# Sampled tokens of both recurrent branches stacked by heads into 128-row blocks, their new states from sequence-masked values in four row groups

## The reference, cut to what matters

```
# GLA:  S_t = diag(a_t) S_{t-1} + k_t^T v_t ; o_t = q_t S_t
o = einsum(qc * exp(b), S) + einsum(A, vc)
S = exp(b_last) * S + einsum('bhsd,bhsv->bhdv', kc * exp(b_last - b), vc)
# GDN:  S_t = g_t (I - b_t k_t k_t^T) S_{t-1} + b_t k_t v_t^T ; o_t = q_t S_t
X = triangular_solve(L, rhs)           # L is 4 x 4 for a sampled sequence
v_new = u - einsum(w, S)
o = einsum(qc * exp(b), S) + einsum(attn, v_new)
S = exp(b_last) * S + einsum('bhsd,bhsv->bhdv', kc * exp(b_last - b), v_new)
```

## Time and profile before

| | |
|---|---|
| timed runs, median | 1013.75 us |
| profiled execution, span from first to last instruction | 1005.3 us |
| profiled execution beyond its span | not on the page; the median is 8.45 us above the span |
| TensorE busy | 919.8 us (91%) |
| VectorE, ScalarE, GpSimd busy | 411.9, 261.1, 64.0 us |
| GLA's sampled states, TensorE 283.0 to 307.1 us | granted clock 0.50 |
| GDN's sampled states, TensorE 593.2 to 617.5 us | granted clock 0.50 |
| DMA | 190.64 MB, mean 190 GB/s |

### The profile page before, as it was taken

The page is one execution under the profiler, slowest core; times in us unless marked ns, Lnnn a source line. Parts: engine busy times, 40 slices in busy tenths (PEclk is TensorE's granted clock), DMA queues, the critical chain, the costliest instruction groups (busy, mean ns, idle before and its releaser), DMA issues.

```text
span 1005.3 us, 13130 instructions
## 1 busy us (share of the span) xinstructions
PE 919.8 (91%) x5070; PEld 640.2 (64%) x5070; DVE 411.9 (41%) x1038; ACT 261.1 (26%) x630; POOL 64.0 (6%) x92
## 2 busy tenths in 40 slices
PE   5989999989989899999999978958999999999994
PEld 3567767767667699878987777746445444544533
DVE  2120015666655864645555477141132232222215
ACT  3121015666603323343335220130110111011012
POOL 0000000000230000000001056000000000000000
PEclk9879999999957999999999975985999999999998
DMA  8945757252438212131216317990799999997621
GB/s 222 348 155 188 244 173 238 93 168 84 126 129 257 76 43 81 47 125 43 84 43 166 100 42 233 339 349 1 266 339 352 372 337 342 345 378 274 223 112 48
DMA packets 134414, 190.64 MB, mean 190 GB/s; under 512 B 6656, under 2 KB 90283, under 8 KB 134309
## 3 DMA queue, kind: packets, MB, share of 16 engines
q1 hardware_dynamic: 134360, 189.89, 55.8%
HBM read 178.93 MB, written 10.95 MB: 189 GB/s over the span
## 4 chain that ended last, share of the span: by engine, by line
PE 83%; DVE 8%; ACT 3%; issue 2%; SPq 1%; DMA 1%; POOL 0%; DVEq 0%; ACTq 0%; POOLq 0%
PE bank L420 80%; PE bank L423 3%; DMA arena<-in_w_ada 1%; DVE arena L1183 1%; DVE arena L1651 1%; DVE arena L1047 1%; ACT arena L1749 0%; SPq L2136 0%; DVE arena L1168 0%; DVE arena L1337 0%; POOL arena L2094 0%; DVE arena L1432 0%; DVE arena L1429 0%; DVE arena L1474 0%; ACT arena L1923 0%
## 5 line engine op out<-in xcount | busy, mean ns | idle before, releaser
L420 PE MATMUL bank<-arena 128*128 128x288 f32 (+10 forms) x4752 | 877.9, 404 | 65.8 <-DVE arena L1071 8.6
L420 PEld LDWEIGHTS bank<-arena 128*128 128x128 f32 (+5 forms) x4752 | 603.7, 176 | 324.7 <-issue 186.3
L1846 ACT ACTIVATE arena<-arena 128x288 f32<-128x288 f32 (+1 forms) x56 | 25.0, 447 | 157.8 <-DVE arena L1168 157.7
L423 PE MATMUL bank<-arena 128*128 128x128 f32 (+6 forms) x318 | 50.8, 293 | 15.4 <-DMA arena<-in_w_conv 7.4
L423 PEld LDWEIGHTS bank<-arena 128*128 128x128 f32 (+6 forms) x318 | 37.0, 151 | 35.6 <-issue 20.1
L1658 DVE TENSOR_TENSOR arena<-arena,bank 128x288 f32<-128x288 f32 x64 | 28.8, 455 | 29.4 <-PE bank L420 27.9
L1183 DVE SCALAR_TENSOR_TENSOR arena<-arena 128x312 f32<-128x312 f32 x72 | 39.5, 549 | 2.5
L1038 DVE TENSOR_TENSOR arena<-bank,arena 128x18 f32<-128x18 f32 x24 | 4.2, 174 | 82.3 <-PE bank L420 82.3
L1638 DVE SCALAR_TENSOR_TENSOR arena<-bank,arena 128x512 f32<-128x512 f32 x8 | 5.5, 692 | 78.0 <-ACT arena L1994 78.0
L1744 ACT ACTIVATE arena<-arena 128x288 f32<-128x288 f32 (+4 forms) x60 | 33.7, 562 | 2.0
L1984 ACT ACTIVATE arena<-bank 128x512 f32<-128x512 f32 x8 | 4.8, 597 | 111.7 <-PE bank L420 111.7
(11 more groups left out here) (204 smaller groups left out, 465.0 us busy)
## 6 DMA issues: line engine op xcount, KB each, us to landing
arena<-in_w_in SPq DMA_DIRECT2D x36, 1024.0 KB, 6.4
arena<-in_w_exp_gate SPq DMA_DIRECT2D x8, 4096.0 KB, 13.9
arena<-in_w_exp_up SPq DMA_DIRECT2D x8, 4096.0 KB, 17.1
arena<-in_w_exp_down SPq DMA_DIRECT2D x8, 4096.0 KB, 12.8
arena<-in_w_ada SPq DMA_DIRECT2D x24, 1024.0 KB, 5.4
arena<-in_state_gla SPq DMA_DIRECT2D x4, 1024.0 KB, 6.4
out_gla_s<-arena SPq DMA_DIRECT2D x4, 1024.0 KB, 6.7
arena<-in_w_out SPq DMA_DIRECT2D x4, 1024.0 KB, 6.0
```

The lines of the kernel that those rows point to most:

```text
L420: return T.matmul(out, lhsT, rhs, start=start, stop=stop)
L423: return T.transpose(out, in_, ident[0:n, 0:n])
L1846: A.activation(sg, sg, ACT.Exp).then_inc(mark("proj_by_scalar", f"sig{s3}"), 1)
```

## The change

Sampled tokens are stacked by heads: row 32h + t of a 128-row block is token t of head h. GLA needs one such block, GDN two (heads 0 to 3 and 4 to 7). VectorE writes the values of tile 2 straight into that form as it drains the transposes. Scores, solve and outputs become full 128 x 128 products under the block mask `tri4`; the gates are stacked once, at step 3 (`stack`). The old states are read as before, but their result is already in the stacked form, so no expansion is needed, and GLA's output product adds onto it in its bank.

New states: not the keys but the values are masked, once per sequence and side by side (`vM` on GpSimd for GLA, `RM` on VectorE for GDN); a product takes 32 rows of keys of one head (rows 32h to 32h+31, so each head has its own row group) and 512 columns of masked values (two GLA or four GDN sequences), and each head has its own bank.

The order changes too. GLA's tile 2 stands at the steps 28, 29, 30, 32 to 35 (four chunks of two sequences), 36 and 37; each chunk reads two sequences' states and updates them at once, and its state block is loaded there, one by one, not four together. GDN's state updates stand in an item of their own, `gdns_states`, behind the turn, at 74.

```diff
-GLA_AT = ((21, 22, 23, 23, 24, 25), (25, 26, 27, 27, 28, 29), (29, 30, 31, 33, 34, 35))
-GDN_AT = (38, 53, 68)
+GLA_AT = ((21, 22, 23, 24, 25), (25, 26, 27, 28, 29))
+GLAS_AT = (28, 29, 30, 32, 33, 34, 35, 36, 37)
+GDN_AT = (38, 53)
+GDNS_AT = 68
+STACK_AT = 3
...
-        elif item == ("gla_states_read", 2):
-            for i in range(4):
-                add(("sgla", i), I["state_gla"][2 * i:2 * i + 2].rearrange("s h k v -> k (s h) v"))
+        elif kind == "glas_chunk":
+            add(("sgla", c), I["state_gla"][2 * c:2 * c + 2].rearrange("s h k v -> k (s h) v"))
...
-                for s in range(NSEQ):
-                    pe.wait_ge(*when(f"kem1 {s}"))
-                    for g in range(2):
-                        b = take(6 + g, f"gla state {s} {g}")
-                        for hh in range(2):
-                            h = 2 * g + hh
-                            last = mm(b[:, 256 * hh:256 * hh + 256], kem1[0:32, s % 2, 128 * h:128 * h + 128],
-                                      vA[0:32, 2, 256 * h:256 * h + 256])
...
+        def glas_decays():
+            pe.wait_ge(*when("wa2"))
+            b = take(4, "gla2 logits read")
+            for h in range(HA):
+                last = mm(b[32 * h:32 * h + 32, 0:DKA], raT[0:RANK + 1, SEQ:TOK],
+                          wa2[0:RANK + 1, DKA * h:DKA * h + DKA])
...
+        def glas_chunk(c):
...
+            for q in range(2):
+                s_ = 2 * c + q
+                for h in range(HA):
+                    mm(pm[6][32 * h:32 * h + 32, 0:DVA], qbM[:, h, 32 * s_:32 * s_ + 32], w[:, q, h, :],
+                       s_ == 0, False)
+            pe.wait_ge(*when(f"vM {c}"))
+            for h in range(HA):
+                b = take((4, 5, 7)[h], f"gla state {c} {h}") if h < 3 else ring_bank(f"gla state {c}")
+                mm(b[:, 0:512], keTa[32 * h:32 * h + 32, 0, :],
+                   vM[32 * h:32 * h + 32, 2 * c:2 * c + 2, :].rearrange("p s v -> p (s v)")) \
+                    .then_inc(mark("gla_products", f"gla state product {c} {h}"), 1)
...
+        def gdns_states():
+            pe.wait_ge(*when("gdn2 ke"))
+            for half in range(2):
+                for g in range(2):
+                    pe.wait_ge(*when(f"RM {half} {g}"))
+                    for j in range(4):
+                        b = take(4 + j, f"gdn state {half} {g} {j}")
+                        mm(b[:, 0:512], ke[32 * j:32 * j + 32, g, :],
+                           RM[2 * half + g][32 * j:32 * j + 32].rearrange("p s v -> p (s v)")) \
+                            .then_inc(mark("gdn_products", f"gdn state product {half} {g} {j}"), 1)
...
+        def glas_scores():
+            pool.wait_ge(*when("gla1 oT1 ready"))
+            pool.wait_ge(*when("vtok7"))
+            for s in range(NSEQ):
+                ins = G.tensor_scalar(vM[:, s, :], vAS, const("seq")[:, s:s + 1], None, ALU.mult)
+                if s % 2:
+                    ins.then_inc(mark("masked_values", f"vM {s // 2}"), 1)
...
+            if name[0] == "sgla":
+                for h in range(HA):
+                    sp.wait_ge(*when(f"gla state {c} {h}"))
+            else:
                 for g in range(2):
-                    sp.wait_ge(*when(f"{name[0][1:]} state {s} {g}"))
+                    for j in range(4):
+                        sp.wait_ge(*when(f"gdn state {c // 2} {g} {j}"))
```

More of the change, by code:

```diff
@@ L334, in used @@
         return f"used {chunk_of[name]}"
[L339 to L343, removed]
+    GLA_PARTS = ("decays", "sums", "scores", "out", "turn")
+    GLAS_PARTS = [("glas_decays",), ("glas_sums",), ("glas_scores",)] + [("glas_chunk", c) for c in range(4)] \
+        + [("glas_out",), ("glas_turn",)]
+    GDN_PARTS = [("gdn_scores",)] + [("gdn_level", lv) for lv in range(LEVELS)] \
+        + [("gdn_values",), ("gdn_out",), ("gdn_turn",)]
+    GDNS_PARTS = [("gdns_scores",), ("gdns_level", 0), ("gdns_level", 1), ("gdns_values",), ("gdns_out",),
+                  ("gdns_turn",), ("gdns_states",)]
     stands_after = {}
@@ L846, in gdn_turn, with gdns_scores @@
                 last.then_inc(mark("gdn_products", t + f"oT{g} ready"), 1)
+        def gdns_scores():
+            pe.wait_ge(*when("gdn2 tg"))
+            b = take(4, "gdn2 D")
+            mm(b[:, 0:2 * P], ones, X2[:, 0:2, :].rearrange("p g t -> p (g t)")) \
+                .then_inc(mark("gdn_products", "gdn2 bc"), 1)
+            pe.wait_ge(*when("gdn2 compact"))
+            b = take(6, "gdn2 KK read")
+            for g in range(2):
+                last = mm(b[:, P * g:P * g + P], kC[:, g, :], kC[:, g, :])
+            last.then_inc(mark("gdn_products", "gdn2 KK"), 1)
+            b = take(5, "gdn2 AT")
+            for g in range(2):
+                last = mm(b[:, P * g:P * g + P], kC[:, g, :], qC[:, g, :])
+            last.then_inc(mark("gdn_products", "gdn2 QK"), 1)
@@ new lines, in gdns_out, with gdns_turn @@
+        def gdns_out():
+            pe.wait_ge(*when("gdn2 vn"))
+            b = take(4, "gdn2 o")
+            for g in range(2):
+                last = mm(b[:, P * g:P * g + P], AT[:, g, :], R[:, g, :])
+            last.then_inc(mark("gdn_products", "gdn2 o ready"), 1)
+        def gdns_turn():
+            pe.wait_ge(*when("gdn2 oN"))
+            b = take(4, "gdn2 oT1")
+            for g in range(2):
+                last = tr(b[:, P * g:P * g + P], Y[:, g, :], P)
+            last.then_inc(mark("gdn_products", "gdn2 oT1 ready"), 1)
@@ L1910, in gla_out, with gdns_out @@
+        def gdns_out():
+            act.wait_ge(*when("gdn2 o"))
+            for g in range(2):
+                last = A.activation(sqo[:, g, :], E[:, g, :], ACT.Square, accum_out=ssum[:, g:g + 1])
+            last.then_inc(mark("gdn_by_scalar", "gdn2 squares"), 1)
+            act.wait_ge(*when("gdn2 squares"))
+            rstd(srs[:, 0:2], ssum[:, 0:2], 1.0 / DVB, "gdn_by_scalar", "gdn2 rstd")
         def gla_out(m):
```

549 lines of the change are left out of this document (340 added, 209 removed).

## The result

The changed kernel takes 963.8 us (median of four runs, 962.3 to 964.3) against 1013.3 beside it: a ratio of 0.952, 95% interval 0.950 to 0.954. The forecast was 967.

What follows compares the result with a forecast made beforehand. TensorE, busy 919.8 of 1005.3 us, was taken as the bound. GLA -30, GDN -1.4 and -15.4, gates and constants +0.3 sum to -46.5: span 958.8, plus 8.45 gives 967 us; 8-in-10 range 957 to 988.

Steps and rivals of the forecast that it cites:

- A chunk: GLA steps 33 to 36, each with a chunk before it: TensorE 6.8 us, VectorE 6.6, four times 6.8 making 27.2.
- The open choice: Chunk state passes: 3.46 us one after the other or 0.87 four at once; 0.87 taken from the column groups.
- the new wait for bank 4: GLA step 28: sampled decays wait until 234.5 for VectorE to empty the bank, with step 29 queued behind.
- the start of the first chunk: GLA after steps 30 to 32: TensorE at 258.5, with nothing won yet against the old kernel.
- the fold's wait for VectorE: GLA steps 30 and 31: GpSimd's masks cost VectorE 2 to 3 us; bound 0 to 2, nothing in the sum.
- GDN's scores: After GLA's step 38: VectorE some 4 us behind from chunk 3; scores start at 299.6, 30 us won.
- GDN to the end of the reads: Sampled GDN from scores until reads: 15.8 us instead of 17.2, 1.4 won; the reads stay at 7.2.
- Behind the reads: GDN's reads to the output projection: 30.4 us instead of 45.8, 15.4 won; updates 17.9 of it.
- rivals 2 and 3: Low clock during GLA's chunks, 995 us, chance 0.06; low clock kept from step 32 on, 1032 us, chance 0.03.
- rival 1: GLA and GDN state products: row groups do not overlap, 20 us more, 987 us; chance 0.13.
- SP's queue: Step 36's weights wait for block 0's store, bound 0 to 2; later GDN stores, bound 0 to 3; both taken 0.
- The added 8.45 us: Whole kernel: median of timed runs above the profiled span, added to the predicted span of 958.8 to give 967.

Runs made afterwards that it cites:

- the experiment on one row group: All heads' state products put on rows 0 to 31 instead of four row groups, against the changed kernel: 991.6 us.
- Chunks together: The four GLA chunks placed together behind step 35 instead of one each behind steps 32 to 35, against the changed kernel: 965.0 us.
- the second execution: The changed kernel run once more, unedited, beside three edited kernels on the same chip: 963.6 us (956.3 to 964.2).
- the experiment on the masks: ScalarE instead of GpSimd masks the values of GLA's sampled tokens, against the changed kernel: 960.5 us.
- the output product at 37: GLA's sampled output product behind step 37 instead of 36, its turn behind 38 instead of 37, against the changed kernel: 961.4 us.
- fillers: 22 full-height products of constants put into TensorE's waits in the sampled GDN part, against the changed kernel: 964.7 us.

## Why the prediction was right

The sum was -46.5 us of span, the measured one -44.9. That they lie so near is in part luck: GLA fell short by 4.1 us and GDN's prompt part lost 1.6 that were not in the sum, while the stretch behind the reads gave 1.6 more and the rest 2.2 that nothing predicted. By its steps:

- **A chunk** was to cost TensorE 6.8 us with its step, VectorE 6.6, nearly level with TensorE later. Measured 6.64, TensorE without a gap, VectorE waiting 0.17 us per chunk: right. The open choice, four row groups at once, was right by the experiment on one row group. The eight passes took 1.14 where 0.87 was put; one after the other they take 3.70, a factor of 3.2 (3.0 with the 3.46 of the rate). With the changes of shape they cost 1.2 us (6.64 less 1.00 for the reads and less 4.42 for a step without a chunk, a third of the 13.27 in Chunks together), and 0.87 + 0.35 = 1.2 was put: the passes were put too short and the changes too long, and the two cancel.

  The Trainium skill, TensorE: Matmul & The Clock Gate, Part 3, has 3.07x for this shape, which makes an estimate of 1.13 us from the 3.46. The trace agrees with the page here (1.14), and not with the full factor that I took from the column groups.
- **Ahead of the chunks** the new wait for bank 4 (predicted without a length; measured 1.66) and the wait for the sums (1.1 with its product; 1.03) came as worked out. Mis-sized is the start of the first chunk: 258.5 predicted, 263.56 measured. Of these 5.1 us, 1.26 lie before step 28 and 1.7 in it, at a clock of 0.73. Neither is a price of the change: the wait ahead of step 28 ends between 219.5 and 223.4 us in the thirteen profiles, and the second execution has step 28 at full clock. The mis-sized term is the next, the 1.43 of the fold's wait for VectorE, which I had bounded at 0 to 2 and taken as 0; the experiment on the masks gives GpSimd 0.45 of it. Then 0.43 is the "issue" wait ahead of the chunks, and the remaining 0.3 is in the rates.
- **GDN's scores** were to wait 4.0 us for VectorE, and wait 4.09. The size is right, the reason is not, and that is luck: I put it down to chunk 3, but VectorE had caught up behind it and itself waited 1.98 us for ScalarE's root (294.40). From there it works without a gap for 9.2 us, the work of two convolution steps and the mask product, while TensorE has one turn and one step. On one row group, where VectorE was busy for only 26.59 of the chunks' 43.34 us and waited 6.00 us for that root, the 9.2 us and the wait of 4.09 are the same; with the output product at 37 the wait is 3.93. What I left out is what comes behind it: TensorE then starts GDN at 0.75 where it started at 1.00, and from there to the sampled scores it is 224.4 us where it was 222.8. GLA won 25.9, not 30; counted from the wait ahead of step 28 it won 27.1, and 28.8 in the second execution.
- **GDN to the end of the reads**: 1.4 predicted, 1.5 measured (1.9 before the reads, which then took 7.7 instead of 7.2). **Behind the reads**: 30.4 predicted, 28.8 measured. The updates start 10.0 us after the reads (10.3 predicted), the last stretch to the output projection is 2.2 (2.3 predicted). Off is the round of VectorE, 1.3 us in all: back to back it takes 1.04 us (16.62/16), where the 1.12 of the earlier trace rows was one round standing between two waits.
- **The clock**: 1.00 through the chunks, as said; rivals 2 and 3 did not come. With the state products one after the other (3.70 instead of 1.14 us), in the experiment on one row group, the clock did fall between the chunks, and the single row group cost 28 us where rival 1 had 20.
- **SP's queue** cost nothing, as put: no wait for a store at step 36, none of the output projection for its weights.
- **The rest**: behind the start of the output projection the span is 2.2 us shorter, where nothing was predicted. In the second execution of the changed kernel this part is 0.5 us longer than before, not shorter: it is the spread.
- **The added 8.45 us** were a mistake that did no harm. In every run whose span is on record the time is 1.9 us above it, so 1005.3 is 1007.2 of time, and the profiled execution was 6.5 us faster than the median of 1013.75. With 1.9 the forecast would have been 960.7, against 962.3 and 964.2 for the two profiled executions and 963.8 for the median: as near as 967, on the other side.

## What to carry to other kernels

Products that fill 32 rows are cheap when four heads stand on four row groups with a bank each: three times the rate here, and the clock stays at 1.00 between full-height steps; on one row group they cost their own time and then that of the neighbours. Work of VectorE that nothing depends on belongs beside TensorE's long steps: the state updates left ahead of the merge were 8 us that moving them into the output projection won, once the memory that held its weights was free. Before adding anything to the span of a profiled execution, compare that execution's own time with the median.

## What was not expected of the hardware

- The same instructions behind the same wait run at different clocks from one execution to the next. Step 28 follows a wait of 2.05 to 2.06 us in all thirteen profiles of this study; it took 4.53 us in eight, and 6.1 to 6.2 in five. In the experts, a block of 32 passes takes 7.1 us, but once or twice per execution 8.78, at 0.81:

```profile
926.80:935.58 8.78, 8.78 (x33) 3.20 (x33) 0.69 (x1) 0.00 (x0) 0.00 (x0) 0.81 0.00 0
```

  Steps of 1.7 us like these make up part of a kernel's spread (956.3 to 964.2 for one kernel).
- TensorE waited 2.2 to 2.3 us for "issue" in the reads of GDN's states while 4 MB of weights were in flight. Beside 1 MB it waited 0.25 us in the first execution of the changed kernel and not at all in the second, and 0.14 us at most when the loads came earlier.
- Holding the clock at 0.95 to 1.00 with fillers gained 0.9 us in the output projection: the low clock cost little here, since the others hardly waited for TensorE.
